# A decoder step on one Trainium2 core: the cached-key softmax moved one update earlier, and the cached-value products spread over the last update

## What is computed

```
z = rmsnorm(x) @ w_in                     # q, k, v of group A (8 heads); q, k, v, o of group B (8 heads); gates
# samples, group A: three patterns (window, dilation) of 128 cached positions each, plus the own key
s = einsum('bthd,btjhd->bthj', q, kg) * HEAD_DIM ** -0.5
m = max(s); e = exp(s - m); l = sum(e);  o = einsum('bthj,btjhd->bthd', e, vg) / l
o_a = merge of the three patterns by their denominators
# group B (mLSTM), chunk by chunk of 128 tokens, a state C (64 x 64) and n (64) for each head
num = iw * (C q) + (q k^T * dw) v;  den = iw * (n q) + sum(q k^T * dw);  h = num / max(|den|, exp(-m))
C_new = cw * C + sum ws v k^T
x += concat(rmsnorm_A(o_a), o_gate * rmsnorm_B(h_b)) @ w_out
x += ConvGLU(rmsnorm(x));  x += sigmoid(rmsnorm(x) @ w_ple_gate) * (p @ w_ple_proj)
```

## Time and profile before

| what | us |
|---|---|
| median of 3 runs | 3229.04 (3226.77 to 3229.59) |
| the profiled execution | 3227.93, its span 3226.1 |
| TensorE busy | 3122.2 (97%) |
| VectorE busy | 1857.2 (58%) |
| ScalarE, GpSimd busy | 1028.8, 891.9 |

### The profile page before, as it was taken

One profiled execution on the slowest core, in us unless ns is written; L12 is line 12 of the kernel. 1 busy time (PEld: TensorE's weight loads), 2 busy tenths in 40 slices (PEclk: granted clock), 3 DMA queues, 4 the chain that ended last, 5 costly groups with the idle time before them and its releaser, 6 DMA issues.

```text
span 3226.1 us, 50829 instructions
## 1 busy us (share of the span) xinstructions
PE 3122.2 (97%) x19459; PEld 2854.5 (88%) x19459; DVE 1857.2 (58%) x4365; ACT 1028.8 (32%) x2117; POOL 891.9 (28%) x2029
## 2 busy tenths in 40 slices
PE   7999999899999999999999999999999999999999
PEld 7887777599999999999987777766999999999998
DVE  5676455755555555557477755557555555555663
ACT  4444345533111121115344433454321111111251
POOL 3111122405322333223322210332132324223231
PEclk8999999899999999999999999998999999999999
DMA  5211234612111111110221111346111111111111
GB/s 172 54 47 51 54 74 118 189 49 66 44 48 40 40 66 40 53 40 21 94 71 44 49 48 50 82 132 183 64 40 40 40 66 40 53 40 40 40 37 71
DMA packets 228570, 208.87 MB, mean 65 GB/s; under 512 B 36676, under 2 KB 207620, under 8 KB 226736
## 3 DMA queue, kind: packets, MB, share of 16 engines
q1 hardware_dynamic: 228328, 205.62, 21.3%
HBM read 173.96 MB, written 31.61 MB: 64 GB/s over the span
## 4 chain that ended last, share of the span: by engine, by line
PE 88%; DVE 7%; ACT 2%; issue 1%; POOL 1%; DMA 0%; SPq 0%; DVEq 0%; ACTq 0%
PE ps L888 25%; PE ps L890 24%; PE ps L889 24%; PE ps L1051 2%; PE ps L1022 2%; PE ps L1037 2%; PE ps L1191 1%; POOL wlo L841 1%; PE ps L1254 1%; PE ps L1172 1%; DVE lo L1899 1%; PE ps L1259 1%; PE ps L897 1%; DVE att L2068 1%; DVE att L2057 1%
## 5 line engine op out<-in xcount | busy, mean ns | idle before, releaser
L841 POOL TENSOR_TENSOR wlo<-raw,whi 128x128 fp32r<-128x128 f32 (+3 forms) x1952 | 857.6, 479 | 1835.4 <-ACT whi L1441 1404.3
L888 PE MATMUL ps<-hi,wlo 128*128 128x344 f32 x2880 | 927.8, 322 | 13.7 <-POOL wlo L841 8.1
L890 PE MATMUL ps<-hi,whi 128*128 128x344 f32 x2880 | 922.5, 320 | 0.0
L889 PE MATMUL ps<-lo,whi 128*128 128x344 f32 x2880 | 921.8, 320 | 0.0
L888 PEld LDWEIGHTS ps<-hi,wlo 128*128 128x128 f32 x2880 | 544.4, 189 | 16.1 <-POOL wlo L841 8.7
L890 PEld LDWEIGHTS ps<-hi,whi 128*128 128x128 f32 x2880 | 543.7, 189 | 0.0
L889 PEld LDWEIGHTS ps<-lo,whi 128*128 128x128 f32 x2880 | 542.9, 189 | 0.6
L888 PE MATMUL ps<-whi,lo 128*128 128x512 f32 (+3 forms) x1056 | 413.5, 392 | 4.9 <-POOL wlo L841 4.4
L890 PE MATMUL ps<-whi,hi 128*128 128x512 f32 (+3 forms) x1056 | 390.2, 370 | 0.0
L889 PE MATMUL ps<-wlo,hi 128*128 128x512 f32 (+3 forms) x1056 | 389.2, 369 | 0.0
L2471 DVE TENSOR_TENSOR X<-X,ps 128x344 f32<-128x344 f32 x528 | 268.5, 512 | 184.3 <-PE ps L890 182.5
(11 more groups left out here) (325 smaller groups left out, 3881.4 us busy)
## 6 DMA issues: line engine op xcount, KB each, us to landing
raw<-in_w_up SPq DMA_DIRECT2D x44, 1024.0 KB, 5.1
raw<-in_w_in SPq DMA_DIRECT2D x112, 256.0 KB, 4.3
raw<-in_w_down SPq DMA_DIRECT2D x22, 1024.0 KB, 4.9
kvb<-in_cache_win_k SPq DMA_DIRECT2D x48, 256.0 KB, 3.6
cache<-in_cache_win_v SPq DMA_DIRECT2D x42, 256.0 KB, 4.7
X<-x_scratch SPq DMA_DIRECT2D x4, 2064.0 KB, 12.6
raw<-in_w_out SPq DMA_DIRECT2D x8, 1024.0 KB, 8.8
raw<-in_w_ple_gate SPq DMA_DIRECT2D x8, 1024.0 KB, 5.2
```

What stands on the lines that cost most here:

```text
L841: pool.tensor_tensor(out=wlo[:, s, r], in0=raw[:, s, r], in1=whi[:, s, r].bitcast(F32), op=ALU.subtract).then_inc(w_split, 1)
L888: nc.tensor.matmul(out, a_lo, b_hi, start=first, stop=False)
L889: nc.tensor.matmul(out, a_hi, b_lo, start=False, stop=False)
L890: return nc.tensor.matmul(out, a_hi, b_hi, start=False, stop=last)
```

## The change

- Updates 0 and 1 take 12 key products each (0 to 2 in a chunk by the table `KEYS`), update 2 takes none.
- The softmax moves to update 2: the scores are turned in chunk 0, the maximum taken behind chunk 1, the exponential in ScalarE's chunk 2, the weights behind chunk 3, and they are turned back and copied (six copies in place of three) in chunk 6. TensorE's kq products of chunks 1 and 7 of that update get a wait for VectorE (`sp_max`, `pj_done`), since they share a PSUM bank with the transposes.
- The softmax works in the key buffers in place of the array `lo`. pZ moves to columns of `lo`; GpSimd zeroes it in update 2, ahead of its second group of gate products.
- The value products start in the last update's opening: 2 ahead of the last four transposes of `turn_qk`, 4 ahead of the first kq product, then 3, 2, 2, 2, 2, 2, 1 behind chunks 0 to 6, 2 behind the transposes of the state, and 2 behind `turn_y(2)`. Their order is 0 to 7, 9, 10, 12, 15 to 23, and the four of `LATE` (8, 11, 13, 14) last.
- The loads for the softmax (L731) and all 16 early values move ahead in update 2. The order of the other loads in the last update stays.
- In the last update, the memory steps on VectorE stand one chunk earlier each, and one product of them (`memory_gated`) is apart.

The core of the diff:

```diff
-STRIPS = {2: (0, 1, 2), 3: (3,), 4: (4,), 5: (5,), 7: (6, 7)}
+KEYS = (0, 1, 3, 5, 7, 9, 11, 12, 12)
+def keys_of(q, c):
+    return range(12 * q + KEYS[c], 12 * q + KEYS[c + 1]) if q < 2 else ()
+VALUES = (6, 9, 11, 13, 15, 17, 19, 20, 20)
+LATE = (8, 11, 13, 14)
+ORDER = tuple(i for i in range(3 * NB) if i not in LATE) + LATE
...
-                    for i in range(max(2, NT * h2), NT * (h2 + 1)):
-                        load_keys(i)
-                        if h2 == PAIRS - 2:
-                            for t in STRIPS.get(i - NT * h2, ()):
-                                load_strips(t)
+                    if h2 < 2:
+                        for i in range(max(2, 12 * h2), 12 * (h2 + 1)):
+                            load_keys(i)
+                    else:
+                        sp.wait_ge(*at(kq_used, 3 * NB))
+                        for j in range(3):
+                            sp.dma_start(zb[:, j, :], Zd[j].rearrange("b (h d) -> (b h) d", d=HD)).then_inc(zb_in, 16)
+                        for t in range(NT):
+                            load_strips(t)
...
+                        if q + 2 == PAIRS:
+                            pool.wait_ge(*at(gemm_done, GEMM_IN + (NT + 1) * (2 * PAIRS - 1) + 6))
+                            pool.memset(pZ, 0.0).then_inc(pz_set, 1)
...
+                def sample_values(first, last):
+                    for i in ORDER[first:last]:
+                        pe.wait_ge(*at(v_in[i // 6], 96))
+                        nc.tensor.matmul(ps[0:HD, 6, :].rearrange("p (k n) -> p k n", k=4), weight_place(i), value_place(i),
+                                         start=(i == ORDER[0]), stop=(i == ORDER[-1])).then_inc(v_used, 1)
...
+                                if p + 1 == 2 * PAIRS:
+                                    sample_values(0, 2)
                                 pe.wait_ge(*at(q_evac, turned_value(p, 0)))
...
                     next_products(done[2], ahead_b(q, 0))
+                    if q + 1 == PAIRS:
+                        sample_values(2, VALUES[0])
                     pe.wait_ge(*at(rm_done, 2 * (q + 1)))
...
-                            sample_values(c)
+                            sample_values(VALUES[c], VALUES[c + 1])
                         elif c + 1 < NT:
+                            if q + 2 == PAIRS and c == 0:
+                                pe.wait_ge(*at(sp_max, 1))
+                            elif q + 2 == PAIRS and c == NT - 2:
+                                pe.wait_ge(*at(pj_done, 1))
                             kq(c + 1)
...
+                sample_values(VALUES[NT], VALUES[NT] + 2)
                 pe.wait_ge(*at(n_read, NT * PAIRS))
...
                 turn_y(2)
+                sample_values(VALUES[NT] + 2, 3 * NB)
...
-                            sample_keys(NT * q + c)
+                            for i in keys_of(q, c):
+                                sample_keys(i)
```

More of the change, by code:

```diff
@@ L729, in _ @@
                 sp.wait_ge(*at(z_stored[1], stored_value(last - 2) + 48))
-                for j in range(3):
-                    sp.dma_start(zb[:, j, :], Zd[j].rearrange("b (h d) -> (b h) d", d=HD)).then_inc(zb_in, 16)
                 for x in range(2):
@@ L743, in _ @@
                 sp.wait_ge(*at(yb_stored[1], 16 * last))
+                sp.wait_ge(*at(pj_back, 1))
+                sp.wait_ge(*at(pj_done, 1))
                 for t in range(3):
@@ L1179, in sample_turn @@
                         for r in range(3):
[L1180 removed]
+                            mm = nc.tensor.transpose(ps[:, 0, P + r * HD:P + (r + 1) * HD], sm[:, r * P:(r + 1) * P], ident[0:HD, 0:HD])
                         mm.then_inc(pj_back, 1)
[L1183 to L1191 removed]
                     if q == 0:
@@ L1246, in _ @@
                             kq(c + 1)
-                        if q + 1 == PAIRS and c == 2:
+                        if q + 2 == PAIRS and c == 0:
+                            pe.wait_ge(*at(kq_used, 3 * NB))
+                            for r in range(3):
+                                mm = nc.tensor.transpose(ps[0:HD, 0, (r + 1) * P:(r + 2) * P], sall[:, r, :, :].rearrange("p b h -> p (b h)"), ident[:, :])
+                            mm.then_inc(st_ready, 1)
+                        elif q + 2 == PAIRS and c == NT - 2:
                             sample_turn()
@@ L1699, in _ @@
                     if q + 1 == PAIRS:
-                        act.wait_ge(*at(sp_max, 1))
-                        do(nc.scalar.activation(sm, sm, ACT.Exp, scale=SCALE, bias=small[:, 10:11], accum_out=small[:, 11:12]), sp_exp)
                         output_gates(p)
@@ L1710, in _ @@
                         n = B + 2 * (p + 2)
+                        if q + 2 == PAIRS and c == 2:
+                            act.wait_ge(*at(sp_max, 2))
+                            do(nc.scalar.activation(sm, sm, ACT.Exp, scale=SCALE, bias=small[:, 10:11], accum_out=small[:, 11:12]), sp_exp)
                         if q < 2 and c == 2:
@@ L1756, in _ @@
                 y_root_first(2, 5, NT)
+                act.wait_ge(*at(v_used, 3 * NB))
                 for c in range(3):
@@ L2139, in sample_turned @@
                     dve.wait_ge(*at(pz_set, 1))
+                    wide = P + 4 * NH
                     for r in range(3):
-                        src = ps[:, 7, r * HD:(r + 1) * HD].rearrange("p (b h) -> p b h", b=NB)
-                        own = lof[:, 5632 + r * WA:5632 + r * WA + NB * (HD + NH)].rearrange("p (b x) -> p b x", b=NB)[:, :, 0:NH]
-                        do(v.tensor_copy(own, src), pj_done if r == 2 else None, wait=False)
+                        src = ps[:, 0, P + r * HD:P + (r + 1) * HD].rearrange("p (x y z h) -> p x y z h", x=2, y=2, z=2)
+                        for y in range(2):
+                            a = (6 + y) * TOK + 2 * r * P + 2 * y * NH
+                            own = lof[:, a:a + 2 * wide].rearrange("p (x w) -> p x w", x=2)[:, :, 0:2 * (HD + NH)]
+                            own = own.rearrange("p x (z v) -> p x z v", z=2)[:, :, :, 0:NH]
+                            do(v.tensor_copy(own, src[:, :, y]), pj_done if r == 2 and y == 1 else None, wait=False)
                 ig_, lf_, m0_, m1_ = (mg[:, j:j + 1] for j in range(4))
@@ L2321, in _ @@
                             prepare(c + 1)
+                        if q + 2 == PAIRS and c == 0:
+                            sample_scores()
+                        elif q + 2 == PAIRS and c == NT - 2:
+                            sample_turned()
                         finish(c)
```

63 lines of the change are left out of this document (29 added, 34 removed).

## The result

| what | before | after |
|---|---|---|
| median of the runs, us | 3229.1 (3226.8 to 3229.6) | 3257.9 (3252.3 to 3260.9) |
| the profiled execution (its span) | 3227.93 (3226.1) | 3252.31 (3250.5) |

The ratio of the medians is 1.0089 (95% interval 1.0073 to 1.0105): the changed kernel is 0.9% slower. The prediction had the sign, but 3238 and at most 3247: the time lies outside the range. The profiled execution of after is its fastest; the other three are 4 to 9 us longer.

The account below looks back on a forecast made before the run. TensorE, busy 97% of the span, was taken to bound the kernel. The terms 2 x 3.9 + 2 x 1.2 + 1.0 - 1.1 = +10.1 on 3227.93 gave 3238 us, range 3228 to 3247.

Parts of the forecast that it names:

- Update 0, products: VectorE in update 0: five more key products, 7.1 us, less 3.5 idle, lengthen the chain to the last `finish` by 3.5.
- Update 0, loads: Closer key loads in update 0 add 0.4 us, making the update's term +3.9 in each layer, bounds 3.0 and 4.8.
- Behind update 0: Stretch from update 0's last `finish` to update 1's first: no term, 0; small TensorE waits expected only within update 0.
- third rival: Waits in update 0 and the last update leave TensorE at 0.50 into the out-projection's start: 3246 us; chance 0.16.
- Update 1: Update 1: VectorE's 15.7 us of idle time hides the second key products; 0, at most +0.5.
- Update 2: Update 2: six more transposes on TensorE and 0.4 us of waits on VectorE: +1.2 in each layer, bounds 0.6 and 2.2.
- The walls: Last update: TensorE waits 9.0 and 7.2 us at value 12, little at value 18; last `finish` +3.0 and +1.1.
- second rival: Last update with value groups in time: VectorE alone sets it, last `finish` 8 us sooner per layer; 3218 us, chance 0.14.
- The out-projection: Out-projection's start: late values keep the clock up, first matmuls 0.16 apart instead of 0.28: -2.0 and -2.2 us.
- the clock falls and stays: TensorE stays at 0.50 for the rest of the last update and the out-projection's start: 3246 us; chance 0.16.
- the fill works: Last update's opening waits filled, value groups in time, VectorE alone sets the update: stage -20, 3218 us; chance 0.14.

Follow-up runs that it names:

- experiment 3: Kernel before plus five more products of a key product's shapes in update 0's chunks 1 to 5, without more loads: 3239.1 us, ratio 1.0032.
- experiment 4: Changed kernel with values 16 to 18 loaded ahead of state and output weights, 19 to 23 ahead of the output-gates wait, and finer semaphores: 3238.3 us, 1.0032.
- experiment 5: Changed kernel with loads in their order, but separate semaphores for values 12 to 15, 16 to 18 and 19 to 23: 3244.7 us, ratio 1.0061.
- experiment 7: Changed kernel with one added wait: GpSimd's second weight split of the last update begins after VectorE has normalised y tile 3: 3248.3 us, ratio 1.0058.
- experiment 10: Kernel with key products 8, 16, 0, earlier value loads, finer semaphores and delayed GpSimd split (3218.9 us), now without the four late values: 3224.9 us, ratio 0.9991.
- experiment 6: Changed kernel with earlier value loads and finer semaphores, but no value products in the last update's opening; they stand in its chunks: 3237.6 us, ratio 1.0034.
- experiment 11: Changed kernel with three tiny VectorE products on two SBUF inputs, one ahead of splitting each of y tiles 0, 1 and 2: 3255.2 us, ratio 1.0084.

## Why the prediction was wrong

Three terms failed: the price of the keys' loads in update 0, the stretch behind update 0 that had no term at all, and the out-projection.

- **Update 0, products: right.** Five products less the idle time gave 3.5 us (7.1 less 3.5 is 3.6); experiment 3 has 3.9.
- **Update 0, loads: the term was mis-sized.** "I put 0.4 us on it": the working compared 3.6 us between release and use with 2.7 to 3.8 to the landing and named the query's load ahead of each third, but did not add it up. Behind that load (0.4 us of SyncE's time) the key takes 3.7 to 4.0 more, so each third key is late. The waits are 1.84 and 1.26, and with what follows them the loads cost 2.0 and 1.5 (experiment 3 against the changed kernel). The term was 5.9 and 5.4, above its bound of 4.8.
- **Behind update 0: the missing step.** The prediction had small waits of TensorE there and let them end with the update. The clock falls to 0.50 behind them, at the transposes of the state, for 1.3 and 2.6 us. The third rival named those waits, but looked for their cost in the last update.
- **Update 1: right**, 0. **Update 2: right in size**, +1.0 where +1.2 was said; but the 0.4 us in it for the waits on VectorE are not there: before the kq products of chunks 1 and 7 TensorE idles 0.07 us at most.
- **The walls: right.** Value 12 waits 8.7 and 7.6 us (9.0 and 7.2), value 18 1.7 and 0.7, the way to the last `finish` is 2.4 and 1.4 longer (3.0 and 1.1). Experiments 4 and 5 show both parts of the mechanism, the group and the order of the loads. The 8 us that the second rival gave the update without walls are 6.3 and 4.4 in experiment 4 (50.2 and 52.3 to the last `finish`), 1.7 of the second layer's shortfall being the opening's clock.
- **The out-projection: the clock was right, the stage wrong.** The first matmuls stand 0.16 apart. 4.35 us times 1 - 0.16/0.28 is 1.9 and not 2.0; experiment 7 shows 2.1 and 2.3 for it, experiment 10 2.0 and 1.3. But "behind it the chain to the out-projection is ... 6.8 us now" ended at the first matmul. The chain that a later gate product puts out of step lies behind it: GpSimd's gate of chunk 6 came at 641.26, 1.3 us ahead of the last `finish`, where it came 5.2 ahead before; so both splits ran without a pause, VectorE was held in them, and -4.2 became +3.8. Why the gate is late can be read from the rows, but no run isolates it: `memory_update` stands one chunk earlier, so that chunk 6's `finish` comes 4.9 us ahead of the last one where it came 7.2 ahead, and ScalarE's weight split of 1.90 us (from 638.99) now stands between that `finish` and the gate. The prediction had looked at GpSimd's zeroing only.
- **The median.** Its 5.6 us over the profiled execution have no step. The stretch behind update 0 explains at most 1.4 of them, since that execution had already met the fall there in both layers (29.2 and 30.6, where 30.6 is the longest seen). Two things that it did not meet appear in other traces (below): a fall of the clock in the filled opening, 1.7 us in a layer, and VectorE held in one more place, 3.4 us. Whether they did it stays open, since only one execution is profiled.

By rivals: of "the clock falls and stays" the fall is true, at another place; "the fill works" needed earlier landings, and with these it does (experiment 4), but the filling is not what pays (experiment 6).

## What to carry to other kernels

When work is moved to another stage, price its loads and the queue that issues them with it: a load that waits for a late consumer holds every store behind it, and a second product in a chunk is nearly free only where the loads keep up and the rows show idle time in that very chunk (0.15 us for two such products there, 5.9 and 5.4 for five in a row of chunks). A wait for a group of loads stands as late as its last member. And a TensorE at the low clock is not always a cost: first find the engine that sets the stage. Leaving the opening empty cost nothing, where VectorE sets the pace; in the out-projection, which TensorE sets, the low clock costs some 2 us in a layer.

## What the runs showed of the hardware

- **VectorE held by GpSimd.** The root's first operation, two SBUF inputs of 128x3, met GpSimd's run of splits in eight kernels. 3.7 to 4.5 us into an unbroken run it took 0.28 to 0.53 us (six times in three kernels); 7.2 to 9.4 us into it, it took 5.1 to 7.0 and ended with the run (ten times in five kernels; for experiment 11's small operations see there). The Trainium skill, "SBUF — State Buffer", section "SBUF: two separate sides", says that VectorE with two SBUF inputs and GpSimd share a pair of ports under an exclusive lock, and that the loser is blocked for the whole instruction of the other. The short waits agree; the long ones last over 12 to 17 instructions of GpSimd, and experiment 11 leaves their rule open. That the order of instructions does not decide it shows at another place too: one addition of the embedding in the first layer (two SBUF inputs, inside a run of splits) takes 0.73 to 0.77 us in 13 of the 15 kernels and 4.32 in two, with what follows 3.4 us later. In experiment 4:

```profile
1615.00 4.32 DVE L2565 TENSOR_TENSOR X<-X,wa 128x344 f32<-128x344 f32 x1
```

GpSimd's run of splits ends at 1618.95, 0.4 us ahead of its end.
- **The clock behind small waits falls by chance.** With 12 keys in update 0 (seven kernels, 14 updates) the stretch behind it took 27.9 us five times and 29.2 to 30.6 nine times; with 8 or 10 keys (seven kernels, 14 updates) always 27.9. The length of update 0 does not tell them apart (39.02 with the fall in the changed kernel's first layer, 39.03 without in experiment 4's). In the first layer of the changed kernel TensorE idled 0.52, 1.43 and 1.23 us from 441.9 on, and the clock was 0.50 from 449.9 to 453.1. The filled opening of the last update has such a draw too: in eleven kernels (22 updates) the way from the last `finish` of update 2 to the next took 13.7 us 17 times and 15.4 five times, though TensorE has no wait over 0.8 us there. In experiment 4's second layer:

```profile
2191.30:2194.30 3.00, 3.00 (x5) 0.79 (x4) 2.52 (x5) 2.71 (x10) 0.00 (x0) 0.50 0.57 128
```

One profiled execution shows one draw of each.
